# Expert weights streamed through six whole-matrix slots instead of ten half-matrix slots

## The chip, the cores and the metric

The program runs on one core of one Trainium2 chip. The metric is the device time of one execution in microseconds: 1202.32 us, the median of three runs (1202.01 to 1202.64). Five engines work side by side, each through a list of instructions of its own: TensorE (PE) multiplies matrices, VectorE (DVE) and ScalarE (ACT) work element by element, GpSimd (POOL) builds constants and issues some transfers, SyncE (SP) issues nearly all of them. Semaphores order them. Transfers from the memory outside to the on-chip buffer run on 16 DMA engines.

## The reference

One decoder block for 256 tokens of width 1024 in float32: RMS norm, one wide input product, a Conformer convolution beside sliding-window attention, gates that merge them, an output product and the residual. Then a mixture of 32 experts, of which each token takes four:

```python
logits = (hf @ w_router + b_router).astype(jnp.float32)
top_v, top_e = lax.top_k(logits, TOP_K)
top_w = jax.nn.softmax(top_v, axis=-1)
...
g = xblk @ w_gate[e] + b_gate[e]
u = xblk @ w_up[e] + b_up[e]
g = jnp.minimum(g, SWIGLU_LIMIT)
u = jnp.clip(u, -SWIGLU_LIMIT, SWIGLU_LIMIT)
a = (u + 1.0) * (g * jax.nn.sigmoid(SWIGLU_ALPHA * g))
return a @ w_down[e] + b_down[e]
```

The weighted results of the experts are added to the residual, and a final RMS norm with g_final gives the output. Each expert has three matrices of 1024 x 1024 in float32, 4 MiB each: 96 matrices, 403 MB, each of them read once.

## The kernel before

The run has two parts. The front (norm, input product, convolution, attention, output product, router) reads its weights through a ring of 12 slots of 1 MiB. The expert part takes one expert after the other with 64 token places each: a selection product gathers tokens (L1259), a transpose turns them (L1266), gate and up products (L1287 in `product`, bias products at L1292), the activation on DVE and ACT (L967 to L977, L613 to L632), its transpose (L1324), the down product, and a scatter product into four accumulators Y (L1274). In one round the down product of expert b - 1 stands behind the up product of expert b. The loops of TensorE and SP hold five experts.

The matrices come in halves, pieces of 2 MiB: rows (i p k), so that a partition gets four rows in a row, 16 KB. They go through ten slots, `slots` in the arena, and nearly all of these lie over buffers of the front: the first ten pieces can be fetched one by one as the front lets go of them (`first_piece`, L341), at signals such as `silu_ready`, `piece_done` (one per finished weight piece on TensorE), `mixed_ready` and `x_added`. After that SP waits for `piece_done` of the piece ten before and issues the next (L338). All transfers of one issuing engine wait in the order of their issue on one queue; SP's waits hold up whatever stands behind them. The bias of the down product and the gain g_final are fetched by POOL, the latter once the bias has been used (L451). The last piece comes as two halves with a semaphore each.

The end: the last scatter completes Y, ACT squares it with a running sum (L662), DVE multiplies with the gain (L1024) and takes the reciprocal (L1028), both scale (L1031, L654), and SP stores four parts of 256 KB.

## Time and profile before

| | |
|---|---|
| median of three runs | 1202.32 us |
| profiled execution, its time | 1201.08 us |
| its span, first to last instruction | 1199.2 us |
| mean granted TensorE clock | 0.998 |
| TensorE busy (matmul) | 1123.9 us, 94% |
| DVE, ACT, POOL busy | 326.8, 181.7, 31.3 us |
| moved by DMA | 441.72 MB, mean 368 GB/s |
| transfers of expert weights | 191 of 2048 KB and 2 of 1024 KB |
| front, up to the first gate product | 282.04 us |

A span is one execution. Busy times of different engines overlap, so they don't add up to the span. The granted clock is the share of full speed that TensorE was given; here it is full almost throughout. The mean rate of 368 GB/s is over stages that differ: a table by stretches of time says more than the mean. A wait in the trace names what ended it.

### The profile page before, as it was taken

To read this page: it belongs to the slowest core of one execution; us is meant where nothing else is said; L and a number is where in the kernel's file an instruction comes from. 1 tells how busy PE (TensorE), PEld (TensorE's weight loads), DVE (VectorE), ACT (ScalarE), POOL (GpSimd) and SP (SyncE) were. 2 spreads that over 40 slices of the span, in tenths; PEclk is the share of its full clock that TensorE was granted. 3 is DMA by queue.
4 is the path that set the end of the run, shared out by engine and by line. 5 is a ranking of instruction groups with operands and counts; after the bars stand their busy time and mean duration, and the time that the engine had idled before them with its cause. 6 is when DMAs were issued, how large, how long until landed. Compare 5 with 4: busy or idle time off the path is not lost.

```text
span 1199.2 us, 13847 instructions
## 1 busy us (share of the span) xinstructions
PE 1123.9 (94%) x5307; PEld 521.2 (43%) x5307; DVE 326.8 (27%) x785; ACT 181.7 (15%) x352; POOL 31.3 (3%) x41
## 2 busy tenths in 40 slices
PE   6999999999999999999999999999999999999986
PEld 5888887853433333333333333333333333333332
DVE  2899973424111111111111111111111111111111
ACT  2111365222110101011000001100000000000012
POOL 2340000000000000000000000000000000000000
PEclk9999999999999999999999999999999999999999
DMA  9955433549999999999999999999999999999995
GB/s 290 347 179 173 141 104 146 193 171 369 417 428 428 427 427 428 427 428 428 428 428 428 428 428 428 428 428 428 428 428 428 428 428 428 428 428 428 428 428 212
DMA packets 60919, 441.72 MB, mean 368 GB/s; under 512 B 4023, under 2 KB 33977, under 8 KB 36184
## 3 DMA queue, kind: packets, MB, share of 16 engines
q1 hardware_dynamic: 59920, 439.37, 89.1%
q0 software_dynamic: 624, 1.60, 0.5%
q8 instruction: 23, 0.38, 0.1%
q10 hardware_dynamic: 344, 0.30, 0.1%
q14 instruction: 8, 0.07, 0.0%
HBM read 440.08 MB, written 1.05 MB: 368 GB/s over the span
## 4 chain that ended last, share of the span: by engine, by line
PE 57%; DMA 41%; ACT 1%; DVE 1%; issue 0%; SPq 0%; ACTq 0%
DMA arena<-in_w_down 40%; PE bank L1287 27%; PE bank L1074 17%; PE bank L1274 3%; PE bank L1184 2%; PE bank L1259 2%; PE bank L1324 1%; DMA arena<-in_x 1%; PE bank L1266 1%; PE bank L1331 1%; PE bank L1292 1%; PE bank L1097 1%; PE bank L1123 0%; PE bank L1112 0%; PE bank L1301 0%
## 5 line engine op out<-in xcount | busy, mean ns | idle before, releaser
L1287 PE MATMUL bank<-arena 128*64 128x512 f32 x3072 | 693.0, 595 | 51.8 <-DMA arena<-in_w_up 28.2
L1287 PEld LDWEIGHTS bank<-arena 128*64 128x64 f32 x3072 | 218.5, 137 | 478.4 <-issue 393.9
L1074 PE MATMUL bank<-arena 128*128 128x256 f32 x800 | 176.3, 383 | 0.1
L1074 PEld LDWEIGHTS bank<-arena 128*128 128x128 f32 x800 | 153.1, 192 | 21.5 <-issue 0.7
L732 DVE SCALAR_TENSOR_TENSOR conv_out<-arena,conv_out x240 | 97.1, 483 | 0.2
L957 DVE TENSOR_SCALAR bias_selector<-ones_bf,expert_onehot 96x64 bf16<-96x64 bf16 x32 | 7.6, 237 | 281.6 <-PE bank L1266 281.6
L971 DVE TENSOR_SCALAR conv_out<-bank 128x512 f32<-128x512 f32 x32 | 22.1, 691 | 208.5 <-PE bank L1287 208.5
L975 DVE TENSOR_SCALAR conv_out<-bank 128x512 f32<-128x512 f32 x32 | 22.1, 692 | 197.2 <-PE bank L1287 197.2
L1274 PE MATMUL bank<-arena,conv_out 64*128 64x512 f32 x256 | 63.6, 615 | 0.7 <-ACT arena L617 0.7
L1259 PE MATMUL bank<-x_normed,conv_out 128*64 128x512 f32 x256 | 60.5, 593 | 0.0
L613 ACT ACTIVATE arena<-bank 128x512 f32<-128x512 f32 x32 | 19.1, 597 | 267.8 <-PE bank L1259 267.8
L621 ACT ACTIVATE arena<-conv_out 128x512 f32<-128x512 f32 x32 | 20.2, 630 | 244.5 <-DVE conv_out L971 244.5
L617 ACT ACTIVATE arena<-bank 128x512 f32<-128x512 f32 x32 | 19.1, 598 | 234.8 <-PE bank L1287 234.8
L1259 PEld LDWEIGHTS bank<-x_normed,conv_out 128*64 128x64 f32 x256 | 18.6, 137 | 36.4 <-issue 36.4
L1274 PEld LDWEIGHTS bank<-arena,conv_out 64*128 64x128 f32 x256 | 22.1, 186 | 21.8 <-issue 20.1
L1324 PEld LDWEIGHTS bank<-ident,conv_out 128*128 128x128 f32 x128 | 17.9, 210 | 25.9 <-issue 25.9
L1074 PE MATMUL bank<-conv_out,arena 128*128 128x256 f32 x128 | 29.0, 383 | 0.0
L967 DVE TENSOR_SCALAR conv_out<-slot_iota,ranks,weights 128x128 f32<-128x128 f32 x64 | 19.3, 344 | 34.9 <-PE bank L1331 34.9
L1184 PE MATMUL bank<-arena 128*128 128x512 f32 (+1 forms) x80 | 28.5, 510 | 0.0
L973 DVE TENSOR_TENSOR conv_out<-conv_out,arena 128x512 f32<-128x512 f32 x32 | 22.2, 693 | 22.3 <-ACT arena L621 22.3
L1074 PEld LDWEIGHTS bank<-conv_out,arena 128*128 128x128 f32 x128 | 23.9, 190 | 4.2 <-issue 1.2
L1292 PE MATMUL bank<-conv_w_rows_then_biases,bias_selector 96*64 96x512 bf16 x128 | 25.5, 382 | 0.0
(181 smaller groups left out, 477.3 us busy)
## 6 DMA issues: line engine op xcount, KB each, us to landing
arena<-in_w_gate SPq DMA_DIRECT2D x64, 2048.0 KB, 45.0
arena<-in_w_up SPq DMA_DIRECT2D x64, 2048.0 KB, 44.9
arena<-in_w_down SPq DMA_DIRECT2D x63, 2048.0 KB, 43.1
arena<-in_w_in SPq DMA_DIRECT2D x21, 1024.0 KB, 11.9
arena<-in_w_conv_out SPq DMA_DIRECT2D x4, 1024.0 KB, 5.2
arena<-in_w_attn_out SPq DMA_DIRECT2D x4, 1024.0 KB, 5.0
arena<-in_w_out SPq DMA_DIRECT2D x4, 1024.0 KB, 4.8
arena<-in_w_down SPq DMA_DIRECT2D x2, 1024.0 KB, 43.4
```

Source lines behind the costliest of these rows:

```text
L621: act.activation(sig, gmin, ACT.Sigmoid, scale=ALPHA).then_inc(sig_ready, 1)
L732: ins = dv.scalar_tensor_tensor(dst, src, w, dst, ALU.mult, ALU.add)
L971: dv.tensor_scalar(gmin, A[:], LIMIT, None, ALU.min).then_inc(gmin_ready, 1)
L973: dv.tensor_tensor(gmin, gmin, sig, ALU.mult).then_inc(act_steps, 1)
L975: dv.tensor_scalar(uclip, B[:], LIMIT, -LIMIT, ALU.min, ALU.max).then_inc(act_steps, 1)
L1074: last = pe.matmul(bank[n % 3][:, j * T:(j + 1) * T], w[:, c, j * P:(j + 1) * P], src[:, c, :], start=(c == 0), stop=(c == C - 1))
L1184: last = pe.matmul(bank[RESIDUAL_BANKS[t][part]][:, 0:hi - lo], gates[:, C + 2 * i + k, t * P:(t + 1) * P], by_rows(WOUT0 + i)[:, k, lo:hi ...
L1259: last = pe.matmul(G[h * CAP:(h + 1) * CAP, :], sel[:, t, :], xh[:, t, h * 512:(h + 1) * 512], start=(t == 0), stop=(t == TT - 1))
L1274: last = pe.matmul(Y[t][h][:], swT[rows, t, :], yb[rows, :], start=False, stop=ends)
L1287: last = pe.matmul(dst[h * CAP:(h + 1) * CAP, :], lhs(EROWS * i + k), w[:, k, h * 512:(h + 1) * 512], start=(i == 0 and k == 0), stop=(i = ...
L1292: pe.matmul(dst[h * CAP:(h + 1) * CAP, :], bsel[:], bias[:, h * 512:(h + 1) * 512], start=False, stop=False)
L1324: last = pe.transpose(A[:, k * P:(k + 1) * P], hidden.rearrange("q (p k) -> q k p", k=EROWS)[:, k, :], ident[:])
```

## The change

The slots become six of a whole matrix each (`pairs`, 4 MiB): the arena now holds 12 pieces in place of ten. To make room, the buffers of the front that lay beside the arena (convolution output, keys, values, masks) move into it, and the small tiles of the expert part move out. A gate or up matrix is now laid out with eight consecutive rows to a partition (32 KB), a down matrix as before with two runs of 16 KB. From matrix 18 to matrix 91 one transfer fetches a whole matrix; the matrices before come in parts of one to four rows (`ROW_PARTS`), the last four in halves and, at the very end, quarters. TensorE waits per part (`row_arrived`), and SP refills a part when TensorE has used its rows, in the first round by a count of single rows (`rows_done`).

SP, the first transfers of expert weights and what each waits for. Before, ten of 128x4096 numbers (2 MiB):

```order
L338 DMA arena<-in_w_gate 128x4096 [waits silu_ready,piece_done]
L338 DMA arena<-in_w_gate 128x4096 [waits piece_done]
L338 DMA arena<-in_w_up 128x4096 [waits pv_done,pt_done]
L338 DMA arena<-in_w_up 128x4096 [waits piece_done]
L338 DMA arena<-in_w_gate 128x4096 [waits piece_done]
L338 DMA arena<-in_w_gate 128x4096 [waits mixed_ready,piece_done]
L338 DMA arena<-in_w_up 128x4096 [waits piece_done] x2
L338 DMA arena<-in_w_down 128x4096 [waits piece_done]
L338 DMA arena<-in_w_down 128x4096 [waits x_added,xh_ready]
```

In the changed kernel, the same place:

```order
L393 DMA arena<-in_w_gate 128x4096 [waits s_masked]
L393 DMA arena<-in_w_down 128x4096 [waits piece_done]
L393 DMA arena<-in_w_up 128x4096 [waits piece_done]
L393 DMA arena<-in_w_gate 128x4096 [waits pv_done,pt_done]
L393 DMA arena<-in_w_up 128x4096 [waits piece_done] x2
L393 DMA arena<-in_w_gate 128x4096 [waits piece_done]
L393 DMA arena<-in_w_gate 128x2048 [waits mixed_ready]
L393 DMA arena<-in_w_up 128x2048 [waits piece_done] x2
L393 DMA arena<-in_w_down 128x2048 [waits piece_done] x2
L393 DMA arena<-in_w_gate 128x2048 [waits piece_done]
L393 DMA arena<-in_w_gate 128x2048 [waits parts_done]
L393 DMA arena<-in_w_gate 128x2048 [waits x_added,xh_ready]
```

The first row of the changed list, on silu_ready as before, is left out; with it there are eight transfers of 2 MiB and eight of 1 MiB, 24 MiB in place of 20.

SP's loop in the changed kernel, for three of its six matrices:

```order
L393 DMA arena<-in_w_up 128x8192
L433 REGISTER_ALU
L393 ISA [waits piece_done]
L393 DMA arena<-in_w_down 128x2x4096
L433 REGISTER_ALU
L393 ISA [waits piece_done]
L393 DMA arena<-in_w_gate 128x8192
```

One transfer of 8192 numbers (32 KB) per partition stands where two of 4096 stood.

TensorE, the end of the expert part. Before, with the names of the banks (4 and 5: gate and up and their transposes, 7: down, 0 to 3: Y):

```order
L1287 MATMUL bank7<-arena 64x512 [waits moe_full9]
L1287 MATMUL bank7<-arena 64x512 x7
L1324 MATMUL bank4<-ident,conv_out 128x128 [waits act_ready]
L1324 MATMUL bank4<-ident,conv_out 128x128 x3
L1274 MATMUL bank0<-arena,conv_out 128x512 [waits yb_out]
L1274 MATMUL bank1<-arena,conv_out 128x512
L1274 MATMUL bank2<-arena,conv_out 128x512
L1274 MATMUL bank3<-arena,conv_out 128x512
L1331 MATMUL bank5<-ident,conv_out 128x128 [waits selw_ready]
L1331 MATMUL bank5<-ident,conv_out 128x128
L1287 MATMUL bank7<-arena 64x512 [waits moe_full0,actT_out]
```

In the changed kernel (the down product of expert 30 goes to bank 6):

```order
L1402 MATMUL bank4<-ident,hidden 128x128 [waits act_ready]
L1402 MATMUL bank4<-ident,hidden 128x128 x3
L1409 MATMUL bank5<-ident,select_weighted 128x128 [waits selw_ready]
L1409 MATMUL bank5<-ident,select_weighted 128x128
L1368 MATMUL bank6<-arena,act_columns 64x512 [waits rows_full4_4,actT_out]
L1368 MATMUL bank6<-arena,act_columns 64x512 x7
L1347 MATMUL bank0<-x_block,arena 128x512 [waits yb_out]
L1347 MATMUL bank1<-x_block,arena 128x512
L1368 MATMUL bank7<-arena,x_columns 64x512 [waits rows_full5_0,actT_out]
```

The transposes of expert 31 now stand ahead of the second half of expert 30's down product, and half of that expert's scatter behind expert 31's down product.

The diff, cut to its core; names of buffers that only moved are left out:

```diff
-MSLOTS = 10
-CYCLE = 5
...
+NM = 3 * NE
+PAIRS = 6
+FURTHER_PAIRS = (0, 3, 4)
+LOOP0 = 3
+ROUNDS = PAIRS // 3
...
+def matrix_source(n):
+    if n < 2:
+        return 0, n
+    if n == NM - 1:
+        return NE - 1, 2
+    b, j = divmod(n + 1, 3)
+    return (b, j) if j < 2 else (b - 1, j)
+WHOLES = range(3 * PAIRS, NM - 4)
+ROW_PARTS = {n: [(0, 4), (4, 8)] for n in range(3)}
+ROW_PARTS[3] = [(0, 4), (4, 6), (6, 8)]
+ROW_PARTS[4] = [(4, 8), (0, 2), (2, 4)]
+ROW_PARTS[5] = [(0, 2), (2, 4), (4, 6), (6, 8)]
+ROW_PARTS[6] = [(0, 1), (1, 2), (2, 4), (4, 6), (6, 8)]
+for _n in range(7, 2 * PAIRS):
+    ROW_PARTS[_n] = [(0, 2), (2, 4), (4, 6), (6, 8)]
+ROW_PARTS[NM - 1] = [(0, 4), (4, 6), (6, 8)]
...
+ROWS_USED = {n: (0, 1, 5) if n == 0 else (1, 5) for n in range(PAIRS)}
...
+def parts_of(n):
+    return ROW_PARTS.get(n, [(0, MROWS)] if n in WHOLES else [(0, EROWS), (EROWS, MROWS)])
...
+        assert X0 + PIECE == PAIRS * MATRIX and QT0 + PIECE == ATTN0_ + MATRIX // 2 + EPIECE
...
+        pairs = [part(off, MATRIX) for off in (HT0, 0, ATTN0_, 4 * PIECE, 8 * PIECE, GATES0_)]
...
-        slots = [part(off, EPIECE) for off in (HT0, 10 * PIECE, ATTN0_, 0, 2 * PIECE, QT0, 4 * PIECE, 6 * PIECE,
-                                               8 * PIECE, X0)]
...
+            def load(n, lo, hi, full, e, j):
+                w = t_in[("w_gate", "w_up", "w_down")[j]]
+                at = e if isinstance(e, int) else bass.ds(e, 1)
+                if j < 2:
+                    rows = w.rearrange("e (p k) n -> e p k n", k=MROWS)
+                    dst, src = pairs[n % PAIRS][:, lo * D:hi * D], rows[at, :, lo:hi, :]
+                    src = src.rearrange("p k n -> p (k n)" if isinstance(e, int) else "a p k n -> p (a k n)")
+                elif (lo, hi) == (0, MROWS):
+                    rows = w.rearrange("e (i p k) n -> e p i (k n)", p=P, k=EROWS)
+                    dst, src = pairs[n % PAIRS].rearrange("p (i m) -> p i m", i=EW), rows[at]
+                    if not isinstance(e, int):
+                        src = src.rearrange("a p i m -> p (a i) m")
+                else:
+                    rows = w.rearrange("e (i p k) n -> e i p k n", p=P, k=EROWS)
+                    dst, src = pairs[n % PAIRS][:, lo * D:hi * D], rows[at, lo // EROWS, :, lo % EROWS:(hi - 1) % EROWS + 1, :]
+                    src = src.rearrange("p k n -> p (k n)" if isinstance(e, int) else "a p k n -> p (a k n)")
+                sp.dma_start(dst, src).then_inc(full, 16)
...
+            def refill(n, lo, hi):
+                was = n - PAIRS
+                if was in ROWS_USED and hi - 1 in ROWS_USED[was]:
+                    sp.wait_ge(rows_done, rows_used(was, hi - 1))
+                else:
+                    sp.wait_ge(piece_done, FRONT + EW * was + (hi + EROWS - 1) // EROWS)
+                load(n, lo, hi, rows_full[n % PAIRS, lo], *matrix_source(n))
...
             sp.wait_ge(piece_done, NZ)
-            first_piece(0, silu_ready, 2)
-            first_piece(1, piece_done, CONV0 + 3)
+            first_rows(0, 0, silu_ready, 2)
+            first_rows(0, 4, s_masked, 4)
+            first_rows(4, 4, piece_done, CONV0 + 2)
+            first_rows(1, 0, piece_done, CONV0 + 4)
             sp.wait_ge(pt_done, 12)
-            first_piece(2, pv_done, 4)
-            first_piece(3, piece_done, ATTN0 + 1)
-            first_piece(4, piece_done, ATTN0 + 3)
-            sp.wait_ge(piece_done, ATTN0 + NO)
-            first_piece(5, mixed_ready, NO)
-            first_piece(6, piece_done, WOUT0 + 1)
-            first_piece(7, piece_done, WOUT0 + 3)
-            first_piece(8, piece_done, FRONT)
+            first_rows(2, 0, pv_done, 4)
+            first_rows(1, 4, piece_done, ATTN0 + 2)
+            first_rows(3, 0, piece_done, ATTN0 + NO)
+            first_rows(2, 4, piece_done, ATTN0 + NO)
+            first_rows(5, 0, mixed_ready, NO)
+            first_rows(3, 4, piece_done, WOUT0 + 1)
+            first_rows(3, 6, piece_done, WOUT0 + 2)
+            first_rows(4, 0, piece_done, WOUT0 + 3)
+            first_rows(4, 2, piece_done, FRONT)
+            first_rows(5, 2, piece_done, FRONT)
+            first_rows(5, 4, parts_done, TT)
             sp.wait_ge(xh_ready, 2 * TT)
-            first_piece(9, x_added, 1)
-            ROUND0 = (MSLOTS + LEAD) // MPE
-            with sp.Fori(0, (NE - ROUND0) // CYCLE) as cycle:
-                for r in range(CYCLE):
-                    b = cycle * CYCLE + (ROUND0 + r)
-                    for j in range(MPE):
-                        sp.wait_ge(piece_done, b * MPE + (FRONT - LEAD + j - MSLOTS + 1))
-                        load((ROUND0 + r) * MPE - LEAD + j, b if j < 2 * EW else b - 1, j)
-            m = NE * MPE - EW
-            sp.wait_ge(piece_done, FRONT + m - MSLOTS + 1)
-            load(m, *piece_source(m))
-            sp.wait_ge(piece_done, FRONT + LAST - MSLOTS + 1)
-            for k, half_full in enumerate(last_full):
-                cols = slice(k * EPIECE // 2, (k + 1) * EPIECE // 2)
-                sp.dma_start(moe_slot(LAST)[:, cols], piece_of(*piece_source(LAST))[:, cols]).then_inc(half_full, 16)
+            first_rows(5, 6, x_added, 1)
+            for n in range(PAIRS, WHOLES[0]):
+                for lo, hi in parts_of(n):
+                    refill(n, lo, hi)
+            with sp.Fori(LOOP0, (WHOLES[-1] + 1) // PAIRS) as cycle:
+                for i in range(PAIRS):
+                    b, j = divmod(i + 1, 3)
+                    sp.wait_ge(piece_done, cycle * (PAIRS * EW) + (FRONT + EW * (i - PAIRS) + EW))
+                    load(i, 0, MROWS, rows_full[i, 0], cycle * ROUNDS + (b if j < 2 else b - 1), j)
+            for n in range((WHOLES[-1] + 1) // PAIRS * PAIRS, NM):
+                for lo, hi in parts_of(n):
+                    refill(n, lo, hi)
+            sp.wait_ge(piece_done, FRONT + EW * (NM - 3))
+            sp.dma_start(gfin, t_in["g_final"].partition_broadcast(P)).then_inc(gfin_loaded, 16)
...
-            pool.wait_ge(silu_ready, 2)
-            pool.dma_start(bdown[0:NE, :], t_in["b_down"]).then_inc(bdown_loaded, 16)
-            pool.wait_ge(bdown_used, 1)
-            pool.dma_start(gfin, t_in["g_final"].partition_broadcast(P)).then_inc(gfin_loaded, 16)
+            pool.dma_start(bdown, t_in["b_down"]).then_inc(bdown_loaded, 16)
...
+            def row_arrived(n, row, cycle):
+                if n >= NM:
+                    if row % EROWS == 0:
+                        pe.wait_ge(further_full[EW * (n - NM) + row // EROWS], cycle * 16 + (16 - 16 * NE))
+                elif row in dict(parts_of(n)):
+                    pe.wait_ge(rows_full[n % PAIRS, row],
+                               landed(n, row) if cycle is None else cycle * 16 + (landed(n, row) - 16 * LOOP0))
...
+            gate_product(0, 0)
+            pe.wait_ge(wT_out, 1)
+            up_product(1)
+            gather(1)
+            turn_act(0)
+            turn_weights(0)
+            tokensT(1)
+            for b in range(1, ROUNDS * LOOP0 + 1):
+                round_of(b, 3 * b - 1)
+            with pe.Fori(LOOP0, (NE - 2) // ROUNDS) as cycle:
+                for r in range(ROUNDS):
+                    round_of(cycle * ROUNDS + (r + 1), 3 * (LOOP0 * ROUNDS + r + 1) - 1, cycle)
+            b = NE - 1
+            pe.wait_ge(actT_out, b)
+            gate_product(b, NM - 4)
+            pe.wait_ge(swT_out, b)
+            up_product(NM - 3)
+            down_product(b - 1, NM - 2, dst=G, halves=(0,))
+            turn_act(b)
+            turn_weights(b)
+            down_product(b - 1, NM - 2, dst=G, halves=(1,))
+            pe.wait_ge(yb_out, b)
+            scatter((0,), swT_late, y_late)
+            down_product(b, NM - 1, columns=act_late)
+            scatter((1,), swT_late, y_late)
...
+            dv.wait_ge(y_done, 2)
+            dv.tensor_tensor(ysum[:, 1, 512:], Y[1][1][:], gfin[:, 512:], ALU.mult).then_inc(gain_on, 1)
+            y_rstd(0)
+            half_out(0, 0)
+            half_out(0, 1)
+            sum_of_squares(1)
+            y_rstd(1)
+            half_out(1, 0)
```

## Rows read from the trace of the kernel before

**Rows 1.** Stretches, whole run: us, busy of PE PEld DVE ACT POOL, clock, DMA share, GB/s.
```profile
30.00:50.00 20.00, 20.00 (x95) 17.64 (x94) 14.61 (x37) 2.52 (x6) 3.79 (x2) 1.00 1.09 349
...
200.00:230.00 30.00, 29.69 (x149) 25.33 (x148) 7.93 (x15) 5.04 (x11) 0.00 (x0) 1.00 0.57 210
230.00:260.00 30.00, 30.00 (x107) 19.40 (x106) 11.89 (x15) 10.85 (x10) 0.00 (x0) 1.00 0.43 149
260.00:285.00 25.00, 22.62 (x120) 11.84 (x120) 12.35 (x51) 7.42 (x12) 0.00 (x0) 1.00 0.83 321
285.00:290.00 5.00, 5.00 (x26) 2.03 (x24) 0.62 (x1) 0.00 (x0) 0.00 (x0) 1.00 0.70 216
290.00:300.00 10.00, 10.00 (x45) 4.01 (x42) 2.15 (x4) 1.23 (x2) 0.00 (x0) 1.00 1.01 429
300.00:310.00 10.00, 9.25 (x45) 4.25 (x45) 1.67 (x6) 0.98 (x2) 0.56 (x1) 1.00 1.02 399
310.00:545.00 235.00, 235.00 (x1128) 85.78 (x1126) 40.74 (x90) 25.24 (x45) 0.00 (x0) 1.00 1.01 427
600.00:1150.00 550.00, 504.51 (x2358) 175.61 (x2354) 84.26 (x184) 52.62 (x94) 0.00 (x0) 1.00 1.01 428
```

**Rows 2.** The chain of waits in order of time: start us, us, what.
```profile
356.56 3.58 PE bank L1287 x16
...
382.87 3.58 PE bank L1287 x16
...
548.01 39.34 DMA arena<-in_w_down
587.39 3.65 PE bank L1287 x16
...
1174.69 3.65 PE bank L1287 x16
```

**Rows 3.** Waits of TensorE from 548 us: us in total, times, longest.
```profile
PE bank L1287 <- DMA arena<-in_w_up: 28.2, 40, 1.0
```

**Rows 4.** SP's issues in order of time: start us, us, what, count.
```profile
176.29 27.35 SPq L338 DMA_DIRECT2D arena<-in_w_gate  x2
...
243.01 0.33 SPq L338 DMA_DIRECT2D arena<-in_w_gate  x1
258.50 9.09 SPq L338 DMA_DIRECT2D arena<-in_w_up  x2
271.28 6.93 SPq L338 DMA_DIRECT2D arena<-in_w_down  x2
...
285.88 0.35 SPq L338 DMA_DIRECT2D arena<-in_w_gate  x1
```

**Rows 5.** The front's last signals, instructions in order of time.
```profile
185.71 7.17 PE L1074 MATMUL bank<-conv_out,arena 128*128 128x256 f32 x32
188.84 0.17 DVE L755 TENSOR_TENSOR softmax_sink<-softmax_minus_max,sinks 128x8 f32<-128x8 f32 x1
213.50 27.79 PE L1074 MATMUL bank<-arena 128*128 128x256 f32 x128
```

**Rows 6.** Start of the expert part, instructions in order of time.
```profile
282.04 3.65 PE L1287 MATMUL bank<-arena 128*64 128x512 f32 x16 [0.75 <-issue]
302.08 0.56 POOL L451 DMA_DIRECT2D glu_sigmoid<-in_g_final  x1 [125.09 <-PE bank L1301]
```

**Rows 7.** All DMA packets by size, whole run.
```profile
DMA packets 60919, 441.72 MB, mean 368 GB/s; under 512 B 4023, under 2 KB 33977, under 8 KB 36184
```

**Rows 8.** The end of the run, instructions in order of time.
```profile
1178.27 0.75 PE L1324 MATMUL bank<-ident,conv_out 128*128 128x128 f32 x4
...
1180.95 0.44 PE L1331 MATMUL bank<-ident,conv_out 128*128 128x128 f32 x2
...
1189.11 1.99 PE L1274 MATMUL bank<-arena,conv_out 64*128 64x512 f32 x8 [0.70 <-ACT arena L617]
...
1195.60 0.72 ACT L654 ACTIVATE x_normed<-x_normed,rstds 128x512 f32<-128x512 f32 x1 [0.23 <-DVE rstds L1028]
```

More of the change, by code:

```diff
@@ L29 @@
 SLOTS = 12
+SHIFT = 1
 PIECE = 2048
@@ L179, in over @@
         def over(t, off, *dims):
-            flat = t[:].rearrange("p a b -> p (a b)") if len(t.shape) == 3 else t[:]
+            flat = t[:]
+            if len(t.shape) == 3:
+                flat = flat.rearrange("p a b -> p (a b)")
+            if len(t.shape) == 4:
+                flat = flat.rearrange("p a b c -> p (a b c)")
             n = 1
@@ L1372, in further_block @@
                 scatter()
-                up_product(piece)
+                up_product(NM + 1, b)
                 gather(b + 1)
```

331 lines of the change are left out of this document (148 added, 183 removed).

## The prediction

> **What bounds the kernel now.** I read the mean rates by stretch first, then the chain of waits, then the sync engine's issues, then the last 30 us. A "piece" below is half a weight matrix, 2 MiB, as in the kernel before; the experts have 192 of them.
>
> The stretches [rows 1] cut the run in four. Up to 285 us TensorE is nearly always busy and the DMA engines are not: from 200 us on 210, 149 and 321 GB/s, shares 0.43 to 0.83. They have nothing to fetch, because all of their targets are still in use by the front part. From 290 us on they move 427 to 429 GB/s at a share of 1.01, to about 1180. From 310 to 545 TensorE is busy for all 235 us; from 600 to 1150 for 504.5 of 550. So TensorE limits until about 548 and the transfers limit after it, but they run without a pause in both. The chain of waits says the same [rows 2]: matmuls only, up to 548.00, then long stretches of DMA with a few matmuls between. From 587.39 to 1174.69 that chain advances 587.3 us for 120 pieces: 4.894 us a piece, 29.36 us an expert. Before 548 the same six pieces take TensorE 26.31 us (356.56 to 382.87). TensorE thus has 3.05 us an expert to spare, and its waits are short: 28.2 us for up matrices in 40 waits, none over 1.0 us [rows 3].
>
> The end of the kernel is therefore: the moment from which the stream never pauses, plus the pieces still to come at 4.894 us, plus what follows the last data. A transfer finished earlier in the front is worth its full time; time on TensorE before 1100 us is worth nothing.
>
> **The change, part by part.**
>
> A, two more targets. Before, 10 pieces are under way or landed when the experts begin; now 12 (six matrices). All 12 have to be in before the stream starts for this to pay in full. The release times are those of the trace [rows 4, 5]: the front's signals are unchanged, so the new list goes out at 176.3, 189.0 (masked scores), 192.9 (second conv piece), 213.6 (last conv piece), 213.9, 227.5 and 241.4 twice (second and fourth of the four attention pieces, 6.95 us each from 213.50), then 1 MiB each at 243.0, 258.5, about 263, 267.3, 271.3, 271.6, about 273.5 (router products) and 277.9. I take 4.9 us a piece and 2 us from an issue to its first byte (the issue at 285.88 leaves a stretch of 216 GB/s, 285 to 290 [rows 1]). The queue then empties each time until 271; the last four MiB run back to back from 273.3 and are in at about 283.2. Two pieces: 2 x 4.894 = 9.8 us. At worst, if the last two 1 MiB parts slide behind the stream's start, nothing is lost but order: the bytes count alike once the engines are busy.
>
> B, an earlier first refill. Before, the first refill waits for a whole piece: issue at 285.88 for a gate product that starts at 282.04 [rows 4, 6]. Now rows 0 and 1 of matrix 0 are released singly, 0.9 us a row (3.65 us for four), so refills of 0.5 MiB go out at 283.0 and 283.9 and are in at 287.4, when before nothing had begun. The next MiB follows the half matrix at 285.8 and starts at 287.8, where the stream before started at 287.9. From there each release (287.6, 289.4, 291.1, 292.9, ...) comes before the queue is empty; the closest is that of expert 1's gate matrix, rival 2. The gain is the 1 MiB already in, 2.5 us; bounds 0 (other gaps eat it) and 2.9 (285.88 to 283.0).
>
> C, the final gain vector. Its 0.5 MB transfer is issued at 302.08 and takes part in the stream; 300 to 310 shows 399 GB/s in place of 429 (0.7 us lost) [rows 1, 6], and its own bytes are 1.2 us at 428. Now it is queued behind the last weights and is needed only by the vector engine 10 us later. +1.9 us; bounds 1.2 and 3.
>
> D, packets of 32 KB. A transfer of 2 MiB to 128 partitions is 16 KB per partition: 24735 packets of 8 KB or more for 403 MB [rows 7]. Two rows give what a packet costs apart from its bytes. 1 KB packets: 349 GB/s between 30 and 50 us [rows 1], that is 21.8 GB/s an engine, 46.9 ns a packet. 16 KB packets: 4.894 us for 8 packets an engine, 611.8 ns. The slope is 27.2 GB/s an engine, the rest 9.3 ns a packet. Gate and up of matrices 18 to 91 (49 of these 74) have 8 packets an engine instead of 16: 8 x 9.3 = 74 ns, x 49 = 3.6 us. Down matrices keep 16 KB runs. No row shows a packet over 16 KB, so the bounds are 0 (cut in two, or the 9.3 ns belongs to something else) and 3.6 above; below zero see rival 3. The Trainium skill (DMA: Bandwidth & Descriptors, "Why small descriptors are slow") gives a fixed overhead of about 3 cycles of an 850 MHz fabric, 3.5 ns; by it the sum would hold 1.4 us here in place of 3.6. I keep the trace's two rates, which have 9.3.
>
> E, packets of 8 KB. Matrices 6 to 11 come in two-row parts, 32 packets an engine in place of 16: 6 x 16 x 9.3 ns = 0.9 us lost. (The parts before them land in idle time.)
>
> F, the end. Before: piece 190 (second half of expert 30's down matrix) is released at 1174.69, and the last scatter starts 14.4 us later, at 1189.11 [rows 8]. Now the two transposes of expert 31 stand ahead of that half. TensorE comes to it 3.6 us after the first half's release, which is one piece (4.9 us) earlier, plus 0.75 and 0.44 for the transposes and a gap: 0.2 us late at most; then 3.6 for the half, 0.7 for the copy, 1.0 for half a scatter, 7.1 for expert 31's down matrix, and 1.0 for the other half beside the next copy: 13.6, or 0.8 less, of which I count 0.4 (the rest for gaps). The last megabyte must be in before 1185.5 (by this clock); the transfers are over by 1184. From there to the last scaling the old end takes 7.2 us (1189.11 to 1196.32), a table load among it that goes; in the new order the vector engine does two outputs of tile 0 before it gets to the sum for tile 1, and by the same durations I get 7.0. Together 0.6 us, bounds -1 and 1.5 [rows 2, 8].
>
> Nothing else reaches the path. The bias product that opens Y moves from round 0 to round 1, and the row waits on TensorE find their data long landed. Whole-matrix waits bring TensorE's first wait for data forward: the lead is 13 us longer, 4.3 experts or 113 us of time, and the whole matrix costs 3.6 us of it again (one expert), so TensorE first waits between 630 and 710 us in place of 548. From there a matrix is freed at most some 12 us after it lands, with five more in the queue (49 us): the engines never run dry. It is closest when matrix 12 is used up (382.87 + 16 = 399 us) and matrix 18 can be issued: by then 35 of the 36 pieces issued have landed (16 by 305.0, one per 4.9 us after), which leaves 4 us for the 2 us to the first byte. TensorE alone would end near 1141 (382.87 + 28 x 26.31 = 1119.6 at the end of the rounds, and 22 for the last down matrix, the scatters and the end).
>
> Sum: 9.8 + 2.5 + 1.9 + 3.6 - 0.9 + 0.6 = 17.5 us. The profiled execution took 1201.08 us (span 1199.2 and 1.9 around it), so 1183.6. The median of the three timed runs, 1202.32, lies 1.24 above it; the time that I predict is 1202.32 - 17.5 = 1184.8.
>
> **Rivals.**
> 1. The 32 KB rows bring nothing (cut into 16 KB packets, or the fixed part isn't one per packet). For it: no row has such a packet. Against: two packet sizes fit one line. D is gone: 1188.4.
> 2. The front's end holds the last parts back, or the small refills leave the engines dry for longer. The first 25 us of refills hang on TensorE's pace: two matrices are freed by 296.5, then nothing until expert 1's gate product has done two rows, near 303, first byte near 305; the four pieces last from 285.0 to 305.0. If B is gone and two more gaps of 1.5 us appear: 1184.8 + 2.5 + 3.0 = 1190.3. Against it: the margins are thin but none is negative.
> 3. Slower than before: gate and up rows now lie 32 KB apart, not 16, so the 16 engines read from addresses farther apart, and if these fall on fewer channels of the memory the rate drops in the 49 whole matrices, 480 us of stream. It has 13.9 us (all but D) to eat: it decides from a rate of 416 GB/s, 2.9% down. At 414 it costs 16.2 us: 1204.6. For it: nothing in the rows. Against: the front's loads, of 1 KB pieces out of rows of 21 KB, run at what fits one line with the experts' rate. The Trainium skill has such a rule (DMA: Bandwidth & Descriptors, "Latency and other measured facts"): a row pitch of 512 KiB gave 207 GB/s where a padded one gave 214, and larger powers of two half. By the Trainium skill's 3.3% these matrices would lose 16 us, as at 414, but its pitch is 16 times ours, and no run here shows one.
> 4. The stream isn't what sets the end, because TensorE's rounds with more waits are longer. It would have to lose 40 us in 31 rounds, 1.3 us each; matmul rounds at 26.31 show no sign of it. Then about 1190 or more.
>
> **How the numbers follow.** Forecast 0.63. Rival 1: 0.14. Rival 2: 0.10. Rival 3: 0.07. Rival 4: 0.03. The rest (0.03) is no change from causes that cancel. Low end: all upper bounds, 9.8 + 2.9 + 3.0 + 3.6 - 0.9 + 1.5 = 19.9, 1182.4, and 1 us for the spread between medians and profiled run: 1181. High end: it takes in rivals 1 and 2 and a little of both: 1192. Outside are rivals 3 and the tails. Faster by over 0.2% (2.4 us, about what this measurement can tell from none): 0.90; within 0.03; slower 0.07.
>
> **What would show it.** Gate matrix 0 starts at 282 as before; the first refill is issued near 283.0; no stretch of 10 us after 288 under 420 GB/s; 431 to 432 GB/s where two of three matrices are whole (430.7 in the mean) against 428; TensorE's first wait for data at 630 to 710 us; the last weights landed near 1167; after the last half of expert 30's matrix 14 us to the last scatter. It would be wrong if the mean rate after 400 us stays at 428 or drops, if the DMA engines show gaps between 285 and 400, or if the expert part starts later than 282.

## The result, and the profile after

| | before | after |
|---|---|---|
| median, first group of runs | 1202.16 us (4 runs) | 1183.69 us (1183.01 to 1184.27, 4 runs) |
| median, second group | 1202.18 us (17) | 1182.77 us (1182.02 to 1183.53, 5) |
| span of the profiled execution | 1199.2 us | 1182.1 us |

The ratio in the first group is 0.9846, interval 0.9829 to 0.9863; the second gives 0.9827 (0.9809 to 0.9845). The change is 18.5 us faster in the first group and 19.4 in the second; the spans of the two profiled executions differ by 17.1 us. Predicted: 17.5, and 1184.8 us.

The rates after the change, in the order of [rows 1] (the next to last column is the DMA share, the one ahead of it the granted clock as a share of 2.4 GHz, the last GB/s):

```profile
260.00:285.00 25.00, 22.94 (x122) 12.06 (x122) 12.66 (x51) 7.40 (x12) 0.00 (x0) 1.00 0.81 292
285.00:290.00 5.00, 5.00 (x27) 2.04 (x24) 0.43 (x1) 0.00 (x0) 0.00 (x0) 1.00 1.02 406
290.00:300.00 10.00, 9.74 (x50) 4.23 (x46) 2.56 (x6) 2.10 (x4) 0.00 (x0) 1.00 0.99 391
300.00:310.00 10.00, 9.29 (x46) 3.87 (x47) 2.69 (x8) 0.63 (x1) 0.00 (x0) 1.00 1.02 426
310.00:320.00 10.00, 10.00 (x42) 3.93 (x38) 1.52 (x3) 0.60 (x1) 0.00 (x0) 1.00 1.01 422
320.00:325.00 5.00, 5.00 (x16) 1.46 (x16) 0.00 (x0) 0.00 (x0) 0.00 (x0) 0.66 1.01 416
325.00:330.00 5.00, 5.00 (x27) 2.06 (x24) 0.00 (x0) 0.72 (x2) 0.00 (x0) 1.00 1.00 372
335.00:345.00 10.00, 10.00 (x51) 3.38 (x49) 1.39 (x2) 0.63 (x1) 0.00 (x0) 1.00 0.98 363
345.00:545.00 200.00, 200.00 (x960) 72.34 (x958) 34.85 (x78) 21.81 (x39) 0.00 (x0) 1.00 1.01 431
600.00:1130.00 530.00, 492.17 (x2324) 182.36 (x2320) 84.28 (x184) 51.71 (x92) 0.00 (x0) 1.00 1.00 431
```

The hole at 285 us is nearly closed (406 in place of 216) and the long stretches stand at 431 in place of 428. But between 325 and 345 us the rate is low, though the DMA share reads near 1: a share near 1 doesn't prove a full stream, since the share counts the time that packets took and not their bytes.

The chain of waits, as [rows 2]:

```profile
320.44 8.71 PE bank L1368 x32
...
671.41 49.50 DMA arena<-in_w_down
721.04 7.09 PE bank L1368 x32
...
1130.06 7.09 PE bank L1368 x32
```

TensorE waits for data from 671 us on. From 721.04 to 1130.06 the chain takes 14 experts: 29.216 us each, where [rows 2] have 29.365. The first row, "320.44 8.71", is a down product of 32 matmuls that takes 6.87 us in the next experts (348.60, 374.91 us): here the clock was low.

SP's issues, as [rows 4] (start, us, what, count):

```profile
283.33 6.55 SPq L393 DMA_DIRECT2D arena<-in_w_up  x5
291.28 5.70 SPq L393 DMA_DIRECT2D arena<-in_w_down  x4
302.68 5.70 SPq L393 DMA_DIRECT2D arena<-in_w_gate  x4
309.76 5.70 SPq L393 DMA_DIRECT2D arena<-in_w_up  x4
323.98 5.55 SPq L393 DMA_DIRECT2D arena<-in_w_down  x4
334.47 5.70 SPq L393 DMA_DIRECT2D arena<-in_w_gate  x4
```

Each row is one matrix, 4 MiB, some 9.8 us of stream. The gaps between the rows after 309.76 are 14.2 and 10.5 us: the queue gets its matrices later than the stream could move them. What TensorE does there:

```profile
314.90 1.92 PE L1332 MATMUL bank<-x_normed,select 128*64 128x512 f32 x8
316.75 3.69 PE L1384 MATMUL bank<-conv_w_rows_then_biases,y_block 32*128 32x512 f32 x8
320.38 8.78 PE L1368 MATMUL bank<-arena,act_columns 128*64 128x512 f32 x32
```

The bias product that opens Y (L1384) stands ahead of the down product and is followed by the low clock, at half speed from 321 to 323 us:

```profile
321.00:323.00 2.00, 2.00 (x8) 0.61 (x6) 0.00 (x0) 0.00 (x0) 0.00 (x0) 0.50 1.00 414
```

I call this the clock dip. Last, packets and the end, as [rows 7, 8]:

```profile
DMA packets 56901, 441.69 MB, mean 374 GB/s; under 512 B 4135, under 2 KB 34089, under 8 KB 36520
```

```profile
1159.43 3.65 PE L1368 MATMUL bank<-arena,act_columns 128*64 128x512 f32 x16 [0.23 <-DMA arena<-in_w_down]
...
1172.81 1.88 PE L1347 MATMUL bank<-y_block,scatter 64*128 64x512 f32 x8
...
1178.20 0.72 ACT L730 ACTIVATE x_normed<-x_normed,rstds 128x512 f32<-128x512 f32 x1 [0.23 <-DVE rstds L1085]
```

20381 packets of 8 KB or more, where there were 24735, for nearly the same bytes: packets of over 16 KB exist. Piece 190 (the second half of expert 30's down matrix) comes at 1159.43 in place of 1174.69 (15.26 us), then 13.38 us to the last scatter (14.42 before) and 6.1 to the last scaling's end (7.2 before).

### The profile page after: what moved, and what is told of

Its sections match the earlier page's. It is cut to its first block, busy times and chain, and to the rows that moved or that the text cites. A ratio compares the mean times of both kernels' runs of the same rounds, so it can differ in the third digit from the quotient of the medians.

```text
span 1182.1 us, 13581 instructions
## 1 busy us (share of the span) xinstructions
PE 1119.2 (95%) x5309; PEld 530.7 (45%) x5309; DVE 326.2 (28%) x783; ACT 179.7 (15%) x350; POOL 29.2 (2%) x39
## 4 chain that ended last, share of the span: by engine, by line
PE 90%; DMA 5%; another core or an unknown queue 3%; DVE 1%; ACT 1%; issue 1%; SPq 0%; ACTq 0%; DVEq 0%
PE bank L1368 54%; PE bank L1146 17%; PE bank L1347 5%; PE bank L1332 4%; DMA arena<-in_w_down 4%; PE bank L1256 2%; PE bank L1402 2%; PE bank L1339 1%; PE bank L1375 1%; PE bank L1409 1%; DMA arena<-in_x 1%; PE bank L1169 1%; PE bank L1195 0%; PE bank L1184 0%
## 5 line engine op out<-in xcount | busy, mean ns | idle before, releaser
L1368 PE MATMUL bank<-arena,x_columns 128*64 128x512 f32 x2080 | 468.4, 594 | 26.3 <-DMA arena<-in_w_up 25.0
L1368 PEld LDWEIGHTS bank<-arena,x_columns 128*64 128x64 f32 x2080 | 150.5, 137 | 298.6 <-issue 274.2
L1368 PE MATMUL bank<-arena,act_columns 128*64 128x512 f32 x992 | 220.9, 597 | 13.2 <-DMA arena<-in_w_down 13.2
L1146 PE MATMUL bank<-arena 128*128 128x256 f32 x928 | 204.8, 382 | 0.0
L1146 PEld LDWEIGHTS bank<-arena 128*128 128x128 f32 x928 | 176.4, 191 | 25.8 <-issue 1.7
L1368 PEld LDWEIGHTS bank<-arena,act_columns 128*64 128x64 f32 x992 | 77.4, 138 | 153.5 <-issue 153.5
L794 DVE SCALAR_TENSOR_TENSOR arena<-arena x240 | 97.2, 483 | 0.2
L1347 PE MATMUL bank<-y_block,scatter 64*128 64x512 f32 x248 | 61.5, 614 | 0.0
L1332 PE MATMUL bank<-x_normed,select 128*64 128x512 f32 x256 | 60.7, 592 | 0.0
L684 ACT ACTIVATE y_block<-bank 128x512 f32<-128x512 f32 x31 | 18.5, 597 | 218.1 <-PE bank L1368 218.1
L1035 DVE TENSOR_TENSOR gate_clipped<-gate_clipped,x_block 128x512 f32<-128x512 f32 x32 | 22.2, 693 | 22.2 <-ACT x_block L688 22.2
```

The source lines that it names most:

```text
L794: ins = dv.scalar_tensor_tensor(dst, src, w, dst, ALU.mult, ALU.add)
L1035: dv.tensor_tensor(gmin, gmin, sig, ALU.mult).then_inc(act_steps, 1)
L1146: last = pe.matmul(bank[n % 3][:, j * T:(j + 1) * T], w[:, c, j * P:(j + 1) * P], src[:, c, :], start=(c == 0), stop=(c == C - 1))
L1332: last = pe.matmul(G[h * CAP:(h + 1) * CAP, :], sel[:, t, :], xh[:, t, h * 512:(h + 1) * 512], start=(t == 0), stop=(t == TT - 1))
L1347: last = pe.matmul(Y[t][h][:], sw[rows, t, :], y[rows, :], start=False, stop=ends)
L1368: last = pe.matmul(dst[h * CAP:(h + 1) * CAP, :], lhs(row), rows[:, row, h * 512:(h + 1) * 512], start=(row == 0), stop=(row == MROWS - 1))
```

## The experiments

All are the changed kernel with one edit, except the one on the gain vector. The control is the changed kernel in its two groups, 1183.69 and 1182.77 us. The first four kernels (packet size, held slots, bias product behind) ran in a group where the kernel before took 1201.60, and there the controls scale to 1183.1 and 1182.2; in the other groups it took 1202.15 to 1202.18, as in the controls' own. Every difference is given against both. The first gate product starts anywhere from 281.2 to 283.5 us in the traces, so under about 1 us medians say little, and I rest on rows there. The edits are cut to their core, `...` marks what is left out.

One thing has to be known to read these traces. The clock dip is in the profiled executions of both controls and of the kernel with halves, and behind the moved bias product; it is not in those of the 16 KB rows, the held slots, the coarser refills, the first refill by halves and the old end, though all five have the bias product at its place. So a trace without the dip must be compared with one without it. The kernel of experiment 5 (old end) does that service: up to its last 12 us it is the changed kernel. Its rates, its first gate product and its piece 190:

```profile
325.00:330.00 5.00, 5.00 (x28) 2.19 (x26) 0.41 (x2) 1.20 (x2) 0.00 (x0) 1.00 1.00 416
335.00:345.00 10.00, 10.00 (x50) 3.41 (x48) 1.38 (x2) 0.63 (x1) 0.00 (x0) 1.00 1.02 424
310.00:390.00 80.00, 80.00 (x376) 29.29 (x374) 12.89 (x29) 8.07 (x15) 0.00 (x0) 1.00 1.01 426
```

```profile
283.09 3.65 PE L1362 MATMUL bank<-arena,x_columns 128*64 128x512 f32 x16 [0.42 <-issue]
...
1158.05 3.65 PE L1362 MATMUL bank<-arena,act_columns 128*64 128x512 f32 x16 [0.23 <-DMA arena<-in_w_down]
```

Its issues of the two releases that come late in the control:

```profile
323.23 5.48 SPq L393 DMA_DIRECT2D arena<-in_w_down  x4
333.65 5.70 SPq L393 DMA_DIRECT2D arena<-in_w_gate  x4
```

I call the time from the first gate product to piece 190 the expert time. Here it is 874.96 us; the two controls, with the dip, have 877.21 and 876.70, and the kernel before has 892.65. The low rates at 325 to 345 us (372 and 363 GB/s in the control, 416 and 424 here) thus come with the dip, and it costs 1.7 to 2.2 us. Three other traces without a dip (no bias product, and the two with spread bias products) have 875.0 to 875.9, so a difference of under 1 us of expert time proves nothing.

**1. Packet size.** Halves in place of whole matrices:

```diff
-    return ROW_PARTS.get(n, [(0, MROWS)] if n in WHOLES else [(0, EROWS), (EROWS, MROWS)])
+    return ROW_PARTS.get(n, [(0, EROWS), (EROWS, MROWS)])
...
-                    load(i, 0, MROWS, rows_full[i, 0], cycle * ROUNDS + (b if j < 2 else b - 1), j)
+                    for half in range(EW):
+                        sp.wait_ge(piece_done, cycle * (PAIRS * EW) + (FRONT + EW * (i - PAIRS) + half + 1))
+                        load(i, half * EROWS, (half + 1) * EROWS, rows_full[i, half * EROWS], ...)
```

> The changed kernel, but from matrix 12 on every gate and up matrix comes in two transfers of 2 MiB again: the layout (eight consecutive rows to a partition) is kept, so packets are 16 KB and the rows of two partitions lie 32 KB apart. Packet theory (term D: 9.3 ns fixed for each packet): the rate from 545 us on falls from 430-431 GB/s to 428 and the time rises by 3.6 us against the changed kernel (1187.3). Rival (a packet's size brings nothing over 16 KB): within 1 us of the changed kernel. Rival (32 KB from one row to the next costs rate and the long packets hid it): below 428 GB/s, more than 3.6 us slower. TensorE's first wait for data: later than in the changed kernel (671 us), since a half is used when it lands.

And whole transfers with the old layout:

```diff
-            return flat.rearrange("q (p k) -> q p k", k=MROWS)
+            return flat.rearrange("q (i p k) -> q i p k", p=P, k=EROWS)
...
-                if j < 2:
+                if False:
```

> The changed kernel with its whole 4 MiB transfers, but gate and up laid out as before: half a matrix is 16 KB a partition, so each transfer is made of 16 KB packets at 16 KB from row to row. Everything else is as in the changed kernel. Packet theory: the rate from 545 us on is 428 GB/s and the time 3.6 us above the changed kernel (1187.3). Rival (fewer transfers make the gain, not longer packets): within 1 us of the changed kernel, rate 430-431. With the kernel in halves beside it: if the row distance mattered, that one would be slower than this one by some us; if neither it nor the count of transfers matters, both agree within 1 us.

Measured: 1186.32 us (ratio 0.9858) and 1188.24 (0.9876): 3.2 to 4.1 and 5.1 to 6.0 above the controls. The chain of the kernel with halves, then that with 16 KB rows:

```profile
759.85 49.57 DMA arena<-in_w_down
...
994.76 49.57 DMA arena<-in_w_down
```

```profile
694.01 7.09 PE bank L1369 x32
...
1134.48 7.09 PE bank L1369 x32
```

234.91 us for 8 experts and 440.47 for 15: 29.364 and 29.365 each, exactly as in [rows 2]. So 16 KB packets cost 0.149 us an expert whether a transfer is 2 or 4 MiB and whether rows lie 16 or 32 KB apart. Packet size it is in the long stretch, and neither the number of transfers nor the row distance. The second kernel lost more than this at its start, 225 GB/s in 285 to 290 us, which I didn't pursue. It was no late release: the first refill is issued at 284.04, 1.11 us after its gate product starts, as in the control (283.33 after 282.22). Whether the layout matters for these small parts stays open.

**2. The two added slots.** Matrix 5's four loads held until the experts' first row is used:

```diff
-            first_rows(5, 0, mixed_ready, NO)
...
-            first_rows(5, 2, piece_done, FRONT)
-            first_rows(5, 4, parts_done, TT)
             sp.wait_ge(xh_ready, 2 * TT)
-            first_rows(5, 6, x_added, 1)
...
+            first_rows(5, 0, rows_done, 1)
+            for lo in (2, 4, 6):
+                first_rows(5, lo, rows_done, 1)
```

All four stand behind the other first loads now.

> The changed kernel, but the four loads of matrix 5 (4 MiB, the two added pieces) are held back until the experts' first row has been used (about 283 us); all other loads keep their order and their signals. By term A these 4 MiB are worth 2 x 4.87 us: +9.7 us (1193.4). Rival (the queue would have been kept busy anyway, the two slots only make the stream start fuller): under 3 us. More than 9.7, up to 12, if the DMA engines stand dry from 273 to 285 and a first byte of 2 us is added.

Measured 1191.71 us (0.9905): 8.6 to 9.5 above the controls. From 260 to 285 us it moved 171 GB/s in place of 292; but from 310 to 390:

```profile
310.00:390.00 80.00, 80.00 (x376) 29.29 (x374) 12.80 (x29) 7.79 (x14) 0.00 (x0) 1.00 1.01 425
```

The control has 414 there, but that is its clock dip: this trace has none, and the kernel with the old end, without the dip and with all slots, has 426. So nothing is had back in that stretch. Its first gate product and its piece 190:

```profile
282.69 3.65 PE L1370 MATMUL bank<-arena,x_columns 128*64 128x512 f32 x16 [0.42 <-issue]
...
1167.52 3.65 PE L1370 MATMUL bank<-arena,act_columns 128*64 128x512 f32 x16 [0.23 <-DMA arena<-in_w_down]
```

The expert time is 884.83 us, 9.9 above the 874.96 of the trace with all slots and no dip: the two pieces bring what they were said to.

**3. Where the rate at 325 to 345 goes.** The bias product behind the down product:

```diff
-                if n + 2 == 4:
-                    start_y()
                 down_product(b - 1, n + 2, cycle)
+                if n + 2 == 4:
+                    start_y()
...
```

> The changed kernel, but in round 1 the bias product that opens Y (3.6 us, and a dip of TensorE's granted clock behind it) is issued behind the down product instead of ahead of it. In the changed kernel the stretch 310 to 390 us runs at 414 GB/s, 17 GB/s below the later 431, with one stretch of 20 us at 342 to 403, after a release at 323.98. Thin-queue theory (TensorE's releases come too late there for the queue): the release comes 3 to 5 us earlier, the rate of that stretch rises, and the time falls by 1 to 3 us (1181-1183). Packet theory (the two-row and one-row parts with 8 KB packets lower the rate there): no change, within 0.7 us.

Measured 1182.24 us (0.9825), 0.9 below one control, level with the other. SP's release moved from 323.98 to 318.29 and 310 to 390 rose to 421; 335 to 340 stayed at 356. The dip is in this trace too, again right behind the bias product, which now ends at 327.0:

```profile
328.00:330.00 2.00, 2.00 (x8) 1.16 (x8) 1.09 (x4) 0.55 (x1) 0.00 (x0) 0.50 1.00 418
```

So it went with the products, and the release behind it comes late by it: 333.97 is 52.0 us after the first gate product (281.95), where the trace without a dip has 50.6 (333.65 after 283.09).

Without the bias product at all (`start_y()` taken out; this kernel leaves the bias of the down product out of its result):

> The changed kernel without the bias product that opens Y (its 3.7 us on TensorE and the clock dip behind it, 1.8 us): the down projection's bias is left out of the result. Thin-queue theory: the releases at 323.98 and 334.47 us come 5.5 us earlier, the two low stretches (325-330 and 335-345) fill up, and the time falls by more than with the bias product behind the down product (that gave 1.4 us): 2 to 3 us below the changed kernel. Packet or row-distance theory of the low rate there: within 0.5 us.

Measured 1182.53 us (0.9827); 0.2 to 1.2 below the controls; 310 to 390 at 425, no clock dip. Less than I expected of it. Its expert time is 875.0 us, as with the products in place and no dip (874.96): what costs is the dip, not the 3.7 us of the products. Coarser refills, four rows in place of two for matrices 8 to 11:

```diff
-for _n in range(7, 2 * PAIRS):
-    ROW_PARTS[_n] = [(0, 2), (2, 4), (4, 6), (6, 8)]
+ROW_PARTS[7] = [(0, 2), (2, 4), (4, 6), (6, 8)]
```

> The changed kernel, but matrices 8 to 11 are refilled in two transfers of four rows each (16 KB packets), released by a whole half, in place of four of two rows (8 KB packets), released by two rows. By the cost of a packet (term E, 9.3 ns each): 4 x 16 x 9.3 ns = 0.6 us faster. Thin-queue theory (each release between 302 and 345 us comes only just in time, and a half releases its first two rows 1.75 us later): slower by 1 to 3 us, with lower rates at 318 to 345 us. The changed kernel is 1182.0 after scaling to this group's runs if neither acts.

Measured 1184.32 us (0.9843), 0.6 to 1.6 above the controls: bigger packets didn't pay. It has no dip, and an expert time of 876.33 us, 1.4 above the trace without a dip. It is low where I had said (397 GB/s in 325 to 330, 406 in 335 to 345, where that trace has 416 and 424), and in 300 to 310 too (398). This speaks for late releases, though 1.4 us is little more than two traces can tell.

**4. The first refill by halves.**

```diff
-ROW_PARTS[6] = [(0, 1), (1, 2), (2, 4), (4, 6), (6, 8)]
+ROW_PARTS[6] = [(0, 4), (4, 8)]
```

> The changed kernel, but the first refill (matrix 6) comes in two transfers of four rows, released by whole halves of gate matrix 0, as the kernel before did, in place of one row, one row, and three times two. Term B taken alone: +2.5 us, with 285 to 290 us back near 216 GB/s. Thin-queue theory: what is lost there is partly had back at 335-345 us, where the queue then isn't dry (as in the kernel with 16 KB packets, 425 GB/s from 310 to 390 where the changed kernel has 414): +0.5 to +1.5 us.

```profile
285.00:290.00 5.00, 5.00 (x26) 2.05 (x24) 0.52 (x1) 0.00 (x0) 0.00 (x0) 1.00 0.65 226
310.00:390.00 80.00, 80.00 (x376) 29.17 (x374) 12.25 (x29) 7.78 (x14) 0.00 (x0) 1.00 1.01 426
```

Measured 1185.06 us (0.9851): 1.4 to 2.3 above the controls. The hole at 285 is back, (406 - 226) x 5 / 428 = 2.1 us; against it the next 10 us run at 422 GB/s where the control has 391, 0.7 us. That 310 to 390 has 12 GB/s more than the control's profile is no effect of the edit: this trace has no clock dip, and the one of the old end, without dip, has 426 too. Against that trace the expert time (1159.34 - 282.14 = 877.20 us) is 2.2 longer.

**5. The old end on the scalar and vector engines** (the order of before, with its table load, in the changed kernel):

```diff
+            act.preload_act_table(ACT.Sqrt)
...
-                dv.scalar_tensor_tensor(ysum[:, t, cols], Y[t][h][:], rstd[:, 0, t:t + 1], gfin[:, cols],
-                                        ALU.mult, ALU.mult).then_inc(ysum_ready, 1)
+                    dv.tensor_tensor(ysum[:, t, cols], Y[t][h][:], gfin[:, cols], ALU.mult).then_inc(gain_on, 1)
```

> The changed kernel with the old end on the scalar and vector engines: the table load (1.28 us) ahead of the squares, the gain vector multiplied before the scale, two scalings by the scalar engine. TensorE's order at the end stays new. If the end's gain of 1.84 us is split as the two traces show it, the time from the last scatter to the last scaling goes from 6.14 back to 7.2 us: +1.07 us on the whole kernel. My prediction had 0.2 for this part. If it is +0.2 or less, the gain sits elsewhere.

The kernel with the old end, then the first square of the control:

```profile
1171.43 1.88 PE L1341 MATMUL bank<-y_block,scatter 64*128 64x512 f32 x8
1171.56 1.28 ACT L722 ACT_TABLE_LOAD   x1 [0.37 <-issue]
1172.85 0.60 ACT L728 ACTIVATE gate_clipped<-bank 128x512 f32<-128x512 f32 x1
...
1177.72 0.72 ACT L720 ACTIVATE x_normed<-x_normed,rstds 128x512 f32<-128x512 f32 x1 [0.23 <-DVE rstds L1094]
```

```profile
1173.88 0.60 ACT L725 ACTIVATE gate_clipped<-bank 128x512 f32<-128x512 f32 x1 [1.32 <-PE bank L1347]
```

Measured 1183.54 us (0.9839), from 0.15 below to 0.8 above the controls, so the median doesn't show the 1.07 us expected. The rows do: its last scatter to last scaling is 1178.44 - 1171.43 = 7.0 us, 0.9 more than in the control. The table load ends 1.4 us after the scatter's start, and the first squares wait for it; in the control they start 1.07 us after it. So 0.35 of the 0.9 us is the table load; the rest comes with the changed order, which I didn't split further.

**6. The gain vector alone**, in the kernel before:

```diff
-            pool.dma_start(gfin, t_in["g_final"].partition_broadcast(P)).then_inc(gfin_loaded, 16)
...
+            sp.dma_start(gfin, t_in["g_final"].partition_broadcast(P)).then_inc(gfin_loaded, 16)
```

> The kernel before with one edit: the final gain vector's 0.5 MB transfer is issued by the sync engine behind the last weights in place of by GpSimd at 302 us. Term C alone: 1.9 us faster than the kernel before (bounds 1.2, its own bytes at 428 GB/s, and 3), and 300 to 310 us back from 399 to 428 GB/s. If the transfer cost nothing where it stood: within 0.5 us.

Measured 1201.61 us against 1202.18, ratio 0.9992 (0.998 to 1.0004). Both have some runs near 1205; without these it is 1201.43 against 1201.85. So 0.4 to 0.6 us, which the interval doesn't tell from none. And the stretch from which I had read the loss did not recover, it fell from 399 to 356 GB/s. 308 to 310 us in this kernel, then in the one before:

```profile
308.00:310.00 2.00, 2.00 (x13) 0.85 (x10) 0.00 (x0) 0.00 (x0) 0.00 (x0) 1.00 0.70 147
```

```profile
308.00:310.00 2.00, 2.00 (x12) 0.83 (x10) 0.00 (x0) 0.00 (x0) 0.00 (x0) 1.00 1.12 303
```

SP's issues in the kernel before:

```profile
292.81 3.99 SPq L338 DMA_DIRECT2D arena<-in_w_up  x2
307.71 3.99 SPq L338 DMA_DIRECT2D arena<-in_w_down  x2
```

It has a hole in its weights at 308 to 311 us: the issue at 307.71 comes 11 us after the one before it (the second of the pair that starts at 292.81), and the vector filled part of it. Over 300 to 320 us this kernel moves 382 GB/s, 46 under 428: 2.15 us of stream are missing. The kernel before moves 410, 0.84 us missing, and its 0.52 MB vector is 1.22 us more: 2.06 of weights. Both lose the same.

**7. The bias products spread** over the down product's rows, and the same with the first of them where TensorE waits anyway:

```diff
+                        if opening and row in OPENS:
+                            start_y(*OPENS[row]).then_inc(bias_used, 1)
...
```

> The changed kernel once more, beside the three below, so that they are compared with it on one chip. Two of its four timed runs so far had a mean granted clock of 0.997 and took 0.8 us more than the other two; the kernels with an undisturbed stretch 310 to 390 us (425-426 GB/s) suggest 1182.5 to 1183.3. If the clock dip behind the bias product comes in some executions only, this trace has either 414 GB/s (dip) or about 425 (no dip) there.

> The changed kernel, but the four bias products that open Y (0.9 us each, 32 rows deep) stand one by one behind rows 1, 3, 4 and 6 of round 1's down product in place of all four ahead of it. If a run of 3.7 us of these thin products is what makes the granted clock fall (0.66 in 320-325 us), the dip goes and the stretch 310 to 390 us runs at 425: 1 to 1.6 us below an execution of the changed kernel that has the dip, and all executions alike. If the dip comes from their number and not their standing together, nothing changes against the changed kernel. Thin-queue theory of their place alone: 0 to 0.5 us faster, from the first two rows of the down matrix released 2.8 us earlier.

> As the kernel with the bias products spread, but the first of the four stands where TensorE waits 0.97 us ahead of expert 1's gate product anyway, and the other three behind rows 1, 3 and 5. All later releases of round 1 come another 0.9 us earlier (the gate of expert 2 starts near 331.6 in place of 332.5): if releases still hold the stream anywhere at 325-345 us, up to 0.5 us faster than with the four spread; if not, the same within 0.3 us.

Measured 1182.77 (control), 1182.92 and 1182.84 us. 310 to 390 us in the control, with the bias products spread, and with the first in the gap:

```profile
310.00:390.00 80.00, 80.00 (x368) 29.06 (x366) 12.46 (x29) 7.78 (x14) 0.00 (x0) 0.98 1.01 417
```

```profile
310.00:390.00 80.00, 80.00 (x370) 28.55 (x368) 12.89 (x29) 8.26 (x15) 0.00 (x0) 1.00 1.01 424
```

```profile
310.00:390.00 80.00, 80.00 (x376) 28.21 (x372) 12.59 (x29) 7.78 (x14) 0.00 (x0) 1.00 1.01 425
```

In these two traces there is no dip, and 1.3 to 1.5 us of stream are there that the control lacks. That the edit removed it is not shown: with the products together five of eight traces have no dip either. Nor do the medians show a gain: two of the control's five executions had a mean clock of 0.997, with 1183.53 and 1182.06 us. No version beats the changed kernel by more than can be measured.

## Why the prediction was right, step by step

The frame held: the stream sets the end from the moment it runs without a pause. The predicted signs came: first refill at 283.33 (283.0), 431 GB/s and 29.216 us an expert (430.7), TensorE's first wait at 671 us (630 to 710), 13.4 us from piece 190 to the last scatter (14). The sign "no 10 us stretch under 420 after 288" failed (391 and 363). The 363 goes with the clock dip; the 391 in 290 to 300 us is there without it too (391 in the kernel with the old end).

- **A, two slots, +9.8:** 8.6 to 9.5 by the medians, 9.9 between the two traces without a dip (experiment 2). Mechanism and size held.
- **B, first refill by rows, +2.5:** 1.4 to 2.3 by the medians, 2.2 between the traces without a dip (experiment 4), inside the bounds of 0 to 2.9.
- **C, gain vector, +1.9: wrong in its cause.** Moving it alone brings 0.4 to 0.6 us by the medians, not told from none. The 399 GB/s of [rows 1] was a hole left by a late release, and I read it as a cost of the transfer that lay in it. The changed kernel has 424 GB/s from 300 to 320 where before had 410 of which the vector was part: the same 1.9 us are there. Gate matrix 1 starts at 300.71 in place of 303.87 (the bias product no longer stands ahead of it) and releases come by rows; that these two fill the hole is argued, no run takes them away. The sum was right by luck here.
- **D, packets, +3.6:** 0.149 us an expert by the chains, 9.3 ns for each of 16 packets an engine, as estimated; the medians give 3.2 to 4.1 for the halves. The Trainium skill (DMA: Bandwidth & Descriptors, "Why small descriptors are slow") has a fixed 3 cycles or so per packet, of a fabric at 850 MHz, which I estimate at 0.056 us an expert. The runs show 0.149, so the measurement decides, and the fixed cost goes on from 16 to 32 KB.
- **E, 8 KB packets, -0.9:** not isolated. The kernel with fewer of them was not faster, so their price is smaller than what finer releases bring. By the two rates of term D a stream of 8 KB packets would run at 422 GB/s, an estimate; the trace without a dip has 422 from 300 to 345 us. That fits.
- **F, the end, +0.6: undersized.** It brought 1.84 in the profile: 1.04 between piece 190 and the last scatter (predicted 0.4) and 1.07 from there to the last scaling (predicted 0.2), less 0.27 outside these two. Of the latter, 0.9 is shown by experiment 5: I took the table load for hidden, but the squares waited 0.35 us for it, and the rest came with the old order of gain and scale.
- **The clock dip: not in the prediction.** It costs the control's profile 2.2 us. I had checked the releases up to 305 and at 399 us, and called the bias product's move to round 1 free. The product itself is (experiment 3), but it stands ahead of a close release, and a dip behind it makes that release and the next one 1.6 and 1.7 us later, against the trace without a dip.

Without the dip the change brings 892.65 - 874.96 = 17.7 us of expert time and 1.8 at the end, 19.5 in all. A, B and D make 9.9 + 2.2 + 3.6 = 15.7 of the 17.7, which leaves 2.0 for C and E where I had 1.0, a difference as small as two traces can tell. The profiled execution loses 2.2 to the dip and starts the experts 0.2 later: 17.1. The medians, 18.5 and 19.4, lie between. So the mechanism of the three large terms was right, but that 17.5 came so close is in part luck: F was 1.2 and C with E 1.0 too small, against a dip of 2.2 that I didn't see coming.

**The rivals.** Rival 1 (32 KB rows bring nothing) falls with experiment 1. Rival 2 (thin queue) was partly true and had the wrong place: it names the release near 303, and it was those near 324 and 334, which cost 1.7 to 2.2 us in executions with the clock dip (not 5.5) and nothing that shows in those without. Rival 3 (32 KB pitch) falls: 431 GB/s at 32 KB, and halves at that pitch run as halves at 16 KB. The Trainium skill (DMA: Bandwidth & Descriptors, "Latency and other measured facts") has 207 GB/s at a row pitch of 512 KiB and 214 with a padded one. No such loss shows here at 32 KB. Rival 4 falls: rounds stay at 26.3 us.

## What to carry to other kernels

Time that a transfer takes in a stretch of low rate is not its cost: first ask whether the queue had anything else to move there, by comparing the issue times with the bytes still outstanding. When a stream is let run earlier, its releases can become the bound for a while, so each release after the start wants the same check, not only the first ones: here 1.6 us on one of them was enough to leave the stream thin. Before two traces are compared, look whether both have the same disturbances; the control's dip alone made the held slots and the first refill by halves look as if they had won time back. Longer runs per partition are worth taking while they only change the layout: 9.3 ns a packet, for 16 KB against 32 KB too.

## What the runs showed of the hardware that I had not expected

- TensorE's granted clock fell to a mean of 0.66 in 320 to 325 us (0.50 in 321 to 323, that is 1.2 in place of 2.4 GHz), right behind 3.7 us of products that use 32 of 128 rows, ahead of which it had been busy at full clock; the 32 matmuls behind them took 8.71 us in place of 6.87. Where the products stood behind the down product, it fell behind them there (0.50 in 328 to 330). In other executions it stayed at 1.00: the traces of the old end and four more kernels with the products in place. In none of ten executions with these products spread over the down product was the mean clock under 0.998, but nor was it in the six of the held slots, where they stand together. The kernel before has the same products at 298.08 us with a clock of 1.00. Why it falls in some executions stays open.
- A packet's cost is linear up to 32 KB: 9.3 ns beside its bytes between 1 and 16 KB ([rows 1, 2]) and again between 16 and 32 KB (0.149 us for 16 packets). The fixed part is the same in 2 MiB and 4 MiB transfers (29.364 and 29.365 us an expert).
- Behind the late releases of the control the DMA share still reads 1.00 at 372 and 0.98 at 363 GB/s: the share alone hides a thin queue.
